# Rotary partners by small transfers on the chip in place of a permutation product

## The chip, the cores and the metric

The kernel runs on one core of one Trainium2 chip. The metric is the device time of one execution in microseconds; the time of a kernel is the median of its runs. One further execution was recorded by the hardware profiler; all rows below are from it.

## The reference, cut to what matters

Two transformer layers of width 1024 over 512 positions, the second one's input being the first one's output. The change is in the first layer's second attention branch (`differential_attention`), whose queries and keys, 4 heads with two halves of 64 dims each, get rotary positions in the first 16 of each 64 dims:

```python
def partial_rope(t, cos, sin):
    half = ROT_DIM // 2          # ROT_DIM = 16
    tf = t.astype(jnp.float32)
    t1 = tf[..., :half]
    t2 = tf[..., half:ROT_DIM]
    out = jnp.concatenate([t1 * cos - t2 * sin, t1 * sin + t2 * cos, tf[..., ROT_DIM:]], axis=-1)
    return out.astype(t.dtype)

        qb = partial_rope(q_b.reshape(b, s, 2 * H_B, HEAD_DIM), cos, sin).reshape(b, s, H_B, 2, HEAD_DIM)
        kb = partial_rope(k_b.reshape(b, s, 2 * H_B, HEAD_DIM), cos, sin).reshape(b, s, H_B, 2, HEAD_DIM)
```

The first branch (`chunked_relbias_attention`) has 8 heads in 4 units of two, with a bias by distance (the strips).

## The kernel before

All activations lie with features on the 128 partitions and the 512 positions along the row. A weight panel is 128 output features: it is loaded by SyncE (`load`), rounded on ScalarE to a high part (`split`), its remainder made on VectorE (`low`), and then multiplied in 8 steps of k with three matmuls each (`mm`). The panel's result lies in one of two PSUM banks until ScalarE evicts it (`plain`, `ropein`).

One list, `WORK`, written by `order_of_work`, holds all items, and each engine walks through it and does its own part of each item, in that order, waiting on semaphores. So the list's order is the order on every engine's queue, SyncE's too. `project` puts a panel's matmuls into it, after the fourth of them (`flush_at=3`) what is in `later`, and steps of the side work (`run(side, ...)`) between: with `STEPS_B = 2` one step after the fourth and one after the eighth. The side work is the attention units: `unit_a(0..3)` (first branch), then `unit_b(4..7)` (second). One step of a unit holds, for tile i: `norm` of tile i-1 (VectorE), `value` of tile i-3 (TensorE), two `score` products with their mask (VectorE adds the strip or mask and takes the maximum), two `turn` transposes (TensorE, copied by ScalarE) and two `exp` (ScalarE).

Panels 0 to 11 belong to units 0 to 3. Panels 12 to 23 belong to units 4 to 7, three each: query, key, value. The queries and keys, panels 12, 13, 15, 16, 18, 19, 21 and 22, take the rotary step (`rope_home` names the tile in place of the panel). While they run, the side work is unit 1 (panels 12 to 14), unit 2 (15 to 17) and unit 3 (18 to 23).

The rotary step of panel n stands in `WORK` in the middle of panel n+1, behind `low` of panel n+4:

```python
        n = project("w_in", 8 + u, STEPS_B)
        do("ropein", n)
        later.append(lambda n=n: do("rope", n))
```

TensorE multiplies the evicted panel with a 128 x 128 permutation `perm` that has the partner's place and the sign (line 1194), into a bank of ring T (banks 4 and 5, shared with the turns). VectorE multiplies that bank with the sine's table into a tile g (line 1879), POOL multiplies the panel with the cosine's table (line 2444), and VectorE adds g. The tables `COS` and `SIN` are made beforehand. The strips of the first branch (`strip`) are loaded by SyncE at the start of a unit's first step, and POOL adds the diagonal's mask to them.

Lines: 1194 matmuls, 1197 transposes, 1546 ScalarE's activations, 1879 VectorE's tensor_tensor, 1883 its tensor_scalar, 1978 its mask with maximum, 2444 POOL's tensor_tensor, 2529 SyncE's transfers.

Of the kernel before, what the change touches and what calls it, by code (L numbers as in the profile page):

```python
# [30 lines left out]

C_ID, C_PERM, C_MEAN, C_ONE, C_DIAG = range(5)
G_TRI, G_BLK, G_H0, G_H1, G_INC, G_ID, G_LEV = range(7)
# [3 lines left out]
def shape_constants():  # L37

    p = np.arange(128)[:, None]
    f = np.arange(128)[None, :]  # L40
    c = np.zeros((128, 5, 128), np.float32)
    c[:, C_ID] = p == f

    for base in (0, 64):
        for m in range(8):
            c[base + m + 8, C_PERM, base + m] = -1.0
            c[base + m, C_PERM, base + m + 8] = 1.0
    c[:, C_MEAN] = 1.0 / D
# [24 lines left out]
    inv = (np.float32(500000.0) ** (-np.arange(0, 16, 2, dtype=np.float32) / np.float32(16))).astype(np.float32)  # L73
    freq = np.where(d < 16, inv[d % 8], np.float32(0)).astype(np.float32)[:, None]
    return c.reshape(128, -1), g.reshape(128, -1), strips.reshape(128, -1), freq
# [71 lines left out]
def order_of_work():  # L147
# [4 lines left out]
    def do(*item):  # L152
        work.append(item)
# [175 lines left out]
    for u in range(4, 8):  # L329
        n = project("w_in", 8 + u, STEPS_B)  # L330
        do("ropein", n)
        later.append(lambda n=n: do("rope", n))
        n = project("w_in", 12 + u, STEPS_B)
        do("ropein", n)
        later.append(lambda n=n: do("rope", n))
        n = project("w_in", 16 + u, STEPS_B)
        do("plain", n)
        later.append(lambda u=u: start(side, unit_b, u))
# [308 lines left out]
def at(*item):  # L647

    return RANK[item]
# [43 lines left out]
for _shared, _kinds in SHARED.items():  # L693
    _count = 0
    for _item in WORK:
        for _name in _kinds.get(_item, _kinds.get(_item[0], ())):
# [5 lines left out]
RING_OF = {"panel": "P", "panelb": "P", "score": "S", "babank": "S", "baturn": "S", "vturn": "T", "turn": "T",  # L702
# [113 lines left out]
_at = 0  # L816
for _name, _n in (("soft", 96), ("freq", 1), ("lam", 8), ("lt", 128), ("sub", 1), ("half", 16), ("warm", 1), ("ss", 32),
                  ("ln", 32), ("rms", 16), ("cw", 48), ("rn", 32), ("ba", 32), ("bet", 16), ("al", 16), ("e1", 16),
                  ("w1", 16), ("gg", 16), ("ngc", 16), ("gam", 16), ("kend", 16), ("gend", 32), ("ea", 4), ("tmp1", 16),
                  ("gs", 64), ("nf", 1)):  # L820
    SM[_name] = _at
    _at += _n
# [27 lines left out]
def build(nc, a, out):  # L850

    ctx = ExitStack()
    with ctx:
        def sb(name, shape, dt=F32):
            return ctx.enter_context(nc.sbuf_tensor(name, shape, dt))
# [8 lines left out]
        Wlo = sb("Wlo", [128, HL, 1024], F32R)  # L864
        CC = sb("CC", [128, 5, 128])
        par = sb("par", [128, NP])
# [9 lines left out]

        ident, perm, mean_m, ones, diagm = (CC[:, i, :] for i in (C_ID, C_PERM, C_MEAN, C_ONE, C_DIAG))
        x2_dram = a["x2_scratch"]
# [164 lines left out]
        def let_go(item):  # L1043
# [15 lines left out]
            if kind == "turn":  # L1059
                return [(SG["pt"], at(*item))]  # L1060
            if kind == "rope":
                return [(SG["ropesin"], at(*item))]
            if kind == "feat":
# [126 lines left out]
        def tensor_engine(e):  # L1190
# [8 lines left out]
            def bank_free(*item):  # L1199
                if BEFORE[item] is not None:  # L1200
                    for s, v in let_go(BEFORE[item]):
                        w.wait_ge(s, v)

            for what, *i in WORK:
# [24 lines left out]
                elif what == "vturn":  # L1229
# [7 lines left out]
                    m.then_inc(SG["vturned"], 1)  # L1237

                elif what == "rope":
                    n, = i  # L1240
                    w.wait_ge(SG["ropein"], at("ropein", n))
                    bank_free("rope", n)
                    w.wait_ge(SG["consts"], 80)
                    mm(bank("rope", n), perm, F(rope_home(n))).then_inc(SG["permuted"], 1)

# [296 lines left out]
        def scalar_engine(e):  # L1542
# [9 lines left out]
            for what, *i in WORK:  # L1552
# [61 lines left out]
                elif what == "sin":  # L1614
                    w.wait_ge(*sig("angle", "rest", "sin"))
                    act(F(SIN), F(SIN), ACT.Sin).then_inc(SG["a_small"], 1)

# [256 lines left out]
        def vector_engine(e):  # L1874
# [24 lines left out]
            for what, *i in WORK:  # L1899
# [50 lines left out]
                elif what == "rope":  # L1950
                    n, = i
                    u, j = unit_of(n)
                    f, g = F(HOMES[u][j]), F(39 + at("rope", n) % 2)
                    w.wait_ge(SG["permuted"], at("rope", n))
                    w.wait_ge(*sig("sin", "sin"))
                    tt(g, bank("rope", n), F(SIN), ALU.mult).then_inc(SG["ropesin"], 1)
                    w.wait_ge(SG["ropesin"], at("rope", n))
# [482 lines left out]
        def pool_engine(e):  # L2440
# [9 lines left out]
            for what, *i in WORK:  # L2450
# [7 lines left out]

                elif what == "rope":
                    n, = i  # L2460
                    f = F(rope_home(n))
                    w.wait_ge(SG["permuted"], at("rope", n))
                    w.wait_ge(*sig("cos", "cos"))
                    tt(f, f, F(COS), ALU.mult).then_inc(SG["ropecos"], 1)

                elif what == "merge":
# [58 lines left out]
        def sync_engine(e):  # L2525
# [5 lines left out]
            for what, *i in WORK:  # L2531
# [18 lines left out]
                elif what == "freq":  # L2550
                    dma(SG["consts"], small("freq"), a["freq"])
                    dma(SG["consts"], F(COS).bitcast(I32), a["positions"].partition_broadcast(128))

                elif what == "strip":
# [126 lines left out]
```

## Time and profile before

| | us |
|---|---|
| median of 3 runs | 1491.37 (1489.71 to 1491.49) |
| the profiled execution | 1489.78 |
| its span | 1487.9 |
| TensorE busy | 1454.4 |
| VectorE busy | 815.9 |
| ScalarE busy | 605.9 |
| POOL busy | 135.4 |

The span is from the first to the last instruction; the profiled execution's own time is 1.88 us more. An engine's busy time is the sum of its instructions' time. Idle time is written before an instruction, with what released it. In timelines, instructions of one kind that follow each other are merged into one row with their count. An fp32 product is recorded as two matmuls (a 128 x 128 x 128 transpose too).

### The profile page before, as it was taken

To read this page: it belongs to the slowest core of one execution; us is meant where nothing else is said; L and a number is where in the kernel's file an instruction comes from. 1 tells how busy PE (TensorE), PEld (TensorE's weight loads), DVE (VectorE), ACT (ScalarE), POOL (GpSimd) and SP (SyncE) were. 2 spreads that over 40 slices of the span, in tenths; PEclk is the share of its full clock that TensorE was granted. 3 is DMA by queue.
4 is the path that set the end of the run, shared out by engine and by line. 5 is a ranking of instruction groups with operands and counts; after the bars stand their busy time and mean duration, and the time that the engine had idled before them with its cause. 6 is when DMAs were issued, how large, how long until landed. Compare 5 with 4: busy or idle time off the path is not lost.

```text
span 1487.9 us, 20042 instructions
## 1 busy us (share of the span) xinstructions
PE 1454.4 (98%) x7936; PEld 1155.8 (78%) x7936; DVE 815.9 (55%) x1422; ACT 605.9 (41%) x1096; POOL 135.4 (9%) x112
## 2 busy tenths in 40 slices
PE   7999999999999999999999999899999999999997
PEld 6776677787878888888877777687778888888886
DVE  3544455556575343444467767755664763664463
ACT  4644445542353232322336655224543432442234
POOL 0001100002200000000012000330020110110012
PEclk9999999999999999999999999999999999999999
DMA  6222221213213222232233221100232332222221
GB/s 249 71 93 74 83 68 60 71 57 113 94 40 125 96 99 100 90 108 86 99 116 113 85 72 60 55 31 16 72 114 79 106 110 89 99 100 99 83 74 57
DMA packets 39693, 130.38 MB, mean 88 GB/s; under 512 B 4656, under 2 KB 4912, under 8 KB 39600
## 3 DMA queue, kind: packets, MB, share of 16 engines
q1 hardware_dynamic: 39600, 129.09, 25.3%
q8 instruction: 64, 1.05, 0.3%
q14 instruction: 29, 0.24, 0.1%
HBM read 124.88 MB, written 4.19 MB: 87 GB/s over the span
## 4 chain that ended last, share of the span: by engine, by line
PE 88%; DVE 5%; ACT 3%; issue 2%; DMA 1%; POOL 1%; SPq 0%; POOLq 0%; DVEq 0%; ACTq 0%
PE bank L1194 85%; PE bank L1197 3%; ACT Fm L1546 2%; DVE Fm L1887 1%; DVE Wlo L1879 1%; DVE Fm L1978 1%; ACT Whi L1546 1%; DVE Fm L1879 1%; POOL Fm L2444 0%; DMA Wraw<-in_w_in_dram 0%; DMA Fm<-in_relb_dram 0%; DVE sm L1883 0%; DVE Fm L1883 0%; DVE sm L1887 0%; ACT Xr L1546 0%
## 5 line engine op out<-in xcount | busy, mean ns | idle before, releaser
L1194 PE MATMUL bank<-Rm,Whi 128*128 128x512 f32 x2816 | 872.4, 391 | 0.0
L1194 PEld LDWEIGHTS bank<-Rm,Whi 128*128 128x128 f32 x2816 | 530.8, 189 | 108.7 <-issue 0.7
L1194 PE MATMUL bank<-Rm,Wlo 128*128 128x512 f32 x1408 | 565.3, 401 | 11.8 <-DVE Rm L1879 8.0
L1879 DVE TENSOR_TENSOR Wlo<-Wraw,Whi 128x1024 fp32r<-128x1024 f32 (+1 forms) x224 | 282.4, 1263 | 171.1 <-ACT Whi L1546 170.6
L1194 PEld LDWEIGHTS bank<-Rm,Wlo 128*128 128x128 f32 x1408 | 265.7, 189 | 74.8 <-issue 19.4
L1546 ACT ACTIVATE Whi<-Wraw 128x1024 fp32r<-128x1024 f32 (+1 forms) x224 | 232.8, 1043 | 215.6 <-PE bank L1194 207.6
L1194 PE MATMUL bank<-Xr,Whi 128*128 128x512 f32 x736 | 226.6, 389 | 0.0
L2444 POOL TENSOR_TENSOR Fm<-Fm 128x512 f32<-128x512 f32 (+1 forms) x94 | 126.7, 1357 | 917.6 <-ACT Fm L1546 484.7
L1194 PEld LDWEIGHTS bank<-Xr,Whi 128*128 128x128 f32 x736 | 138.2, 188 | 28.8
L1546 ACT ACTIVATE Fm<-bank 128x512 f32<-128x512 f32 (+4 forms) x200 | 93.0, 483 | 156.0 <-PE bank L1194 105.6
L1194 PE MATMUL bank<-Xr,Wlo 128*128 128x512 f32 x368 | 143.3, 389 | 0.0
L1879 DVE TENSOR_TENSOR Fm<-Fm,bank 128x512 f32<-128x512 f32 (+2 forms) x118 | 75.9, 665 | 122.4 <-PE bank L1194 122.3
L1546 ACT ACTIVATE Fm<-Fm,sm 128x512 f32<-128x512 f32 (+3 forms) x92 | 52.9, 578 | 114.1 <-DVE sm L1883 97.5
L1546 ACT ACTIVATE Fm<-Fm 128x512 f32<-128x512 f32 (+2 forms) x116 | 61.6, 532 | 89.0 <-DVE Fm L1879 48.3
L1194 PE MATMUL bank<-Fm 128*64 128x128 f32 (+7 forms) x848 | 92.9, 318 | 4.1 <-ACT Fm L1546 1.5
L1546 ACT ACTIVATE Fm<-Fm,par 128x512 f32<-128x512 f32 x68 | 50.5, 743 | 102.4 <-DVE Fm L1879 102.4
L1194 PEld LDWEIGHTS bank<-Fm 128*64 128x64 f32 (+3 forms) x848 | 58.1, 155 | 37.8 <-issue 27.5
L1194 PEld LDWEIGHTS bank<-Xr,Wlo 128*128 128x128 f32 x368 | 69.1, 188 | 14.2
L1879 DVE TENSOR_TENSOR Fm<-Fm 128x512 f32<-128x512 f32 x63 | 44.1, 700 | 62.3 <-ACT Fm L1546 56.1
L1879 DVE TENSOR_TENSOR Fm<-bank,Fm 128x512 f32<-128x512 f32 (+1 forms) x65 | 44.4, 686 | 49.9 <-PE bank L1194 47.6
L1887 DVE SCALAR_TENSOR_TENSOR Fm<-Fm,par 128x511 f32<-128x511 f32 x88 | 65.4, 747 | 1.5
L1546 ACT ACTIVATE Rm<-Fm 128x512 fp32r<-128x512 f32 (+1 forms) x58 | 35.9, 626 | 73.1 <-POOL Fm L2444 48.1
(97 smaller groups left out, 755.9 us busy)
## 6 DMA issues: line engine op xcount, KB each, us to landing
Wraw<-in_w_in_dram SPq DMA_DIRECT2D x68, 512.0 KB, 3.2
Wraw<-in_w_ff_dram SPq DMA_DIRECT2D x64, 512.0 KB, 3.2
Wraw<-in_w_up_dram SPq DMA_DIRECT2D x44, 512.0 KB, 3.3
Wraw<-in_w_o_dram SPq DMA_DIRECT2D x16, 512.0 KB, 3.2
Wraw<-in_w_down_dram SPq DMA_DIRECT2D x16, 512.0 KB, 3.2
Wraw<-in_w_ab_dram SPq DMA_DIRECT2D x8, 512.0 KB, 3.3
Wraw<-in_w_down_end_dram SPq DMA_DIRECT2D x8, 384.0 KB, 3.0
Fm<-in_x_dram SPq DMA_DIRECT2D x8, 256.0 KB, 6.1
```

Source lines behind the costliest of these rows:

```text
L1194: return e.matmul(o, l, r, start=first, stop=last)
L1197: return e.transpose(o, x, ident)
L1546: return e.activation(o, x, func, **kw)
L1879: return e.tensor_tensor(o, x, y, op)
L1887: return e.scalar_tensor_tensor(out=o, in0=x, scalar=s, in1=y, op0=op0, op1=op1)
L1978: e.tensor_tensor_reduce(p, bank("score", u, j)[:, 0:n], strip[:, 512 - n:512], 1.0, LOW, ALU.add, ALU.max, mx).then_inc(SG["masked"], 1)
L2444: return e.tensor_tensor(o, x, y, op)
```

## The change

The sign goes from the permutation into the sine: the column `freq` gets a second column with -1 for the first 8 of each 64 dims and 1 elsewhere, which ScalarE's Sin takes as its scale. The partners (rows 0 to 7 from 8 to 15, and back, and the same from 64 on) are copied from the evicted panel's tile to g by four transfers of 8 rows x 512, 16 KB each, issued by SyncE (`ropeswap`), right behind the eviction in `WORK`. g's other rows keep finite values of earlier contents, which meet a sine of zero. VectorE then does all three operations. TensorE's product and POOL's step go, ring T serves the turns alone, and the constants lose one 128 x 128 block. Tiles 39 and 40 alternate as g; they hold angles before, so the first two swaps wait for the sine's table, and later ones for the rotary step two before.

```diff
-C_ID, C_PERM, C_MEAN, C_ONE, C_DIAG = range(5)
+C_ID, C_MEAN, C_ONE, C_DIAG = range(4)
...
-    freq = np.where(d < 16, inv[d % 8], np.float32(0)).astype(np.float32)[:, None]
+    freq = np.stack([np.where(d < 16, inv[d % 8], np.float32(0)), np.where(d < 8, -1, 1)], 1).astype(np.float32)
...
         n = project("w_in", 8 + u, STEPS_B)
         do("ropein", n)
+        do("ropeswap", n)
         later.append(lambda n=n: do("rope", n))
         n = project("w_in", 12 + u, STEPS_B)
         do("ropein", n)
+        do("ropeswap", n)
         later.append(lambda n=n: do("rope", n))
...
-                elif what == "rope":
-                    n, = i
-                    w.wait_ge(SG["ropein"], at("ropein", n))
-                    bank_free("rope", n)
-                    w.wait_ge(SG["consts"], 80)
-                    mm(bank("rope", n), perm, F(rope_home(n))).then_inc(SG["permuted"], 1)
...
-                    act(F(SIN), F(SIN), ACT.Sin).then_inc(SG["a_small"], 1)
+
+                    act(F(SIN), F(SIN), ACT.Sin, scale=small("freq", 1)).then_inc(SG["a_small"], 1)
...
                     f, g = F(HOMES[u][j]), F(39 + at("rope", n) % 2)
-                    w.wait_ge(SG["permuted"], at("rope", n))
-                    w.wait_ge(*sig("sin", "sin"))
-                    tt(g, bank("rope", n), F(SIN), ALU.mult).then_inc(SG["ropesin"], 1)
+                    w.wait_ge(*sig("cos", "cos"))
+                    r = at("rope", n)
+                    w.wait_ge(SG[f"swapped{r % 2}"], 64 * ((r + 1) // 2))
+                    tt(g, g, F(SIN), ALU.mult).then_inc(SG["ropesin"], 1)
+                    tt(f, f, F(COS), ALU.mult).then_inc(SG["ropecos"], 1)
                     w.wait_ge(SG["ropesin"], at("rope", n))
                     w.wait_ge(SG["ropecos"], at("rope", n))
                     tt(f, f, g, ALU.add).then_inc(SG["roped"], 1)
...
-                elif what == "rope":
-                    n, = i
-                    f = F(rope_home(n))
-                    w.wait_ge(SG["permuted"], at("rope", n))
-                    w.wait_ge(*sig("cos", "cos"))
-                    tt(f, f, F(COS), ALU.mult).then_inc(SG["ropecos"], 1)
...
+                elif what == "ropeswap":
+
+                    n, = i
+                    r = at("ropeswap", n)
+                    w.wait_ge(SG["ropein"], at("ropein", n))
+                    if r < 3:
+                        w.wait_ge(*sig("sin", "sin"))
+                    else:
+                        w.wait_ge(SG["roped"], r - 2)
+                    f, g = F(rope_home(n)), F(39 + r % 2)
+                    for to, of in ((0, 8), (8, 0), (64, 72), (72, 64)):
+                        dma(SG[f"swapped{r % 2}"], g[to:to + 8, :], f[of:of + 8, :])
```

On SyncE's queue, from the last constants to the strips of unit 3 (`in_relb` are the strips), before:

```order
L2529 DMA Fm<-in_strips_dram 128x512
L2529 DMA Wraw<-in_w_in_dram 128x1024 [waits s_w_lo,s_w_hi] x4
L2529 DMA Fm<-in_relb_dram 128x512 [waits s_masked]
L2529 DMA Fm<-in_relb_dram 128x512
L2529 DMA Wraw<-in_w_in_dram 128x1024 [waits s_w_lo,s_w_hi] x4
L2529 DMA Fm<-in_relb_dram 128x512 [waits s_masked]
```

The same queue now, the part from the strips of unit 2 to those of unit 3 (swaps of panels 15, 16 and 18):

```order
L2513 DMA Fm<-in_relb_dram 128x512
L2513 DMA Fm<-Fm 8x512 [waits s_roped,s_ropein]
L2513 DMA Fm<-Fm 8x512 x3
L2513 DMA Wraw<-in_w_in_dram 128x1024 [waits s_w_lo,s_w_hi]
L2513 DMA Fm<-Fm 8x512 [waits s_roped,s_ropein]
L2513 DMA Fm<-Fm 8x512 x3
L2513 DMA Wraw<-in_w_in_dram 128x1024 [waits s_w_lo,s_w_hi] x2
L2513 DMA Fm<-Fm 8x512 [waits s_roped,s_ropein]
L2513 DMA Fm<-Fm 8x512 x3
L2513 DMA Wraw<-in_w_in_dram 128x1024 [waits s_w_lo,s_w_hi]
L2513 DMA Fm<-in_relb_dram 128x512 [waits s_masked]
```

The four transfers of a panel stand ahead of the weight load that had followed, and those of panel 18 and one load directly ahead of the strips of unit 3; each group waits for its panel's eviction.

On VectorE's queue, the rotary step of panel 15 with its low half ahead and the norm and masks of unit 2 behind, before:

```order
L1879 TENSOR_TENSOR Wlo<-Wraw,Whi 128x1024 [waits s_w_hi]
L1879 TENSOR_TENSOR Fm<-bank,Fm 128x512 [waits s_permuted]
L1879 TENSOR_TENSOR Fm<-Fm 128x512 [waits s_ropecos,s_ropesin]
L1987 RECIPROCAL sm<-sm 128x2 [waits s_exped]
L1883 TENSOR_SCALAR Fm<-Fm,sm 128x128 [waits s_v_step]
L1883 TENSOR_SCALAR Fm<-Fm,sm 128x128
L1978 ISA Fm,sm<-bank,Fm 128x256 [waits s_turned,s_scored]
```

And now:

```order
L1868 TENSOR_TENSOR Wlo<-Wraw,Whi 128x1024 [waits s_w_hi]
L1868 TENSOR_TENSOR Fm<-Fm 128x512 [waits s_swapped1]
L1868 TENSOR_TENSOR Fm<-Fm 128x512
L1868 TENSOR_TENSOR Fm<-Fm 128x512 [waits s_ropecos,s_ropesin]
L1978 RECIPROCAL sm<-sm 128x2 [waits s_exped]
L1872 TENSOR_SCALAR Fm<-Fm,sm 128x128 [waits s_v_step]
L1872 TENSOR_SCALAR Fm<-Fm,sm 128x128
L1969 ISA Fm,sm<-bank,Fm 128x256 [waits s_turned,s_scored]
```

The step waits for the swap in place of TensorE, and has one operation more, the cosine's product, in place of the wait for POOL.

## Rows read from the trace of the kernel before

**Rows 1.** The page, busy time of each engine (share of the span) and instructions.
```profile
PE 1454.4 (98%) x7936; PEld 1155.8 (78%) x7936; DVE 815.9 (55%) x1422; ACT 605.9 (41%) x1096; POOL 135.4 (9%) x112
```

**Rows 2.** Constants' tile on TensorE, 95 to 200 us: count, ns min/median/max, starts.
```profile
L1194 PE MATMUL bank<-Fm,CC x16: 590/591/697, 99.9 to 191.3; 128*128 128x512 f32 x16
```

**Rows 3.** TensorE's timeline: start, duration (us), work [idle before <-releaser].
```profile
99.89 1.12 PE L1194 MATMUL bank<-Fm,CC 128*128 128x512 f32 x2 [0.41 <-ACT Fm L1546]
...
110.88 0.88 PE L1194 MATMUL bank<-Fm 128*64 128x128 f32 x12
...
125.90 1.02 PE L1194 MATMUL bank<-Fm,CC 128*128 128x512 f32 x2
126.85 0.70 PE L1194 MATMUL bank<-Fm 64*128 64x256 f32 x4
...
130.43 1.22 PE L1194 MATMUL bank<-Fm 64*128 64x384 f32 x4
131.59 0.44 PE L1197 MATMUL bank<-CC,Fm 128*128 128x128 f32 x2
...
135.90 1.12 PE L1194 MATMUL bank<-Fm,CC 128*128 128x512 f32 x2 [1.12 <-ACT Fm L1546]
...
145.99 0.60 PE L1197 MATMUL bank<-CC,Fm 128*128 128x128 f32 x4
...
166.51 1.23 PE L1194 MATMUL bank<-Fm 64*128 64x384 f32 x4
...
171.99 0.66 PE L1197 MATMUL bank<-CC,Fm 128*128 128x128 f32 x4 [1.13 <-ACT Fm L1546]
```

**Rows 4.** ScalarE's timeline, evictions behind the exps.
```profile
107.72 1.33 ACT L1546 ACTIVATE Fm<-bank 128x384 f32<-128x384 f32 x3
...
124.69 0.58 ACT L1546 ACTIVATE Fm<-bank 128x512 f32<-128x512 f32 x1
...
143.73 1.33 ACT L1546 ACTIVATE Fm<-bank 128x384 f32<-128x384 f32 x3
...
151.22 0.60 ACT L1546 ACTIVATE Fm<-bank 128x512 f32<-128x512 f32 x1 [2.12 <-PE bank L1194]
```

**Rows 5.** VectorE's timeline, rotary step of panel 15 and a mask.
```profile
127.38 0.68 DVE L1879 TENSOR_TENSOR Fm<-bank,Fm 128x512 f32<-128x512 f32 x1
128.72 0.69 DVE L1879 TENSOR_TENSOR Fm<-Fm 128x512 f32<-128x512 f32 x1 [0.65 <-POOL Fm L2444]
129.33 0.16 DVE L1987 RECIPROCAL sm<-sm 128x2 f32<-128x2 f32 x1
...
129.92 0.41 DVE L1978 CUSTOM_DVE_ANT_0 Fm<-bank,Fm 128x256 f32<-128x256 f32 x1
...
159.23 0.29 DVE L1978 CUSTOM_DVE_ANT_0 Fm<-bank,Fm 128x128 f32<-128x128 f32 x1 [0.27 <-PE bank L1194]
```

**Rows 6.** SyncE's timeline of transfer issues: two constants, one weight load.
```profile
7.07 0.44 SPq L2529 DMA_DIRECT2D par<-in_par_dram  x1
7.55 0.44 SPq L2529 DMA_DIRECT2D rowp<-in_rows_dram  x1
...
85.84 0.33 SPq L2529 DMA_DIRECT2D Wraw<-in_w_in_dram  x1
```

**Rows 7.** Transfers by source: count, KB each, median us from issue to landing.
```profile
Wraw<-in_w_in_dram SPq DMA_DIRECT2D x68, 512.0 KB, 3.2
...
Wraw<-in_w_down_end_dram SPq DMA_DIRECT2D x8, 384.0 KB, 3.0
...
Fm<-in_relb_dram SPq DMA_DIRECT2D x8, 256.0 KB, 3.9
x_scratch<-Fm SPq DMA_DIRECT2D x8, 256.0 KB, 2.0
...
out_dram<-Fm SPq DMA_DIRECT2D x8, 256.0 KB, 2.5
```

**Rows 8.** Constants' tile on POOL, whole run: the bias strips' masks.
```profile
L2444 POOL TENSOR_TENSOR Fm<-Fm,CC x8: 456/460/913, 34.5 to 157.8; 128x128 f32<-128x128 f32 x8
```

More of the change, by code:

```diff
@@ L40, in shape_constants @@
     f = np.arange(128)[None, :]
-    c = np.zeros((128, 5, 128), np.float32)
+    c = np.zeros((128, 4, 128), np.float32)
     c[:, C_ID] = p == f
[L44 to L47, printed above, removed]
     c[:, C_MEAN] = 1.0 / D
@@ L816 @@
 _at = 0
-for _name, _n in (("soft", 96), ("freq", 1), ("lam", 8), ("lt", 128), ("sub", 1), ("half", 16), ("warm", 1), ("ss", 32),
+for _name, _n in (("soft", 96), ("freq", 2), ("lam", 8), ("lt", 128), ("sub", 1), ("half", 16), ("warm", 1), ("ss", 32),
                   ("ln", 32), ("rms", 16), ("cw", 48), ("rn", 32), ("ba", 32), ("bet", 16), ("al", 16), ("e1", 16),
@@ L864, in build @@
         Wlo = sb("Wlo", [128, HL, 1024], F32R)
-        CC = sb("CC", [128, 5, 128])
+        CC = sb("CC", [128, 4, 128])
         par = sb("par", [128, NP])
@@ L875, in sig @@
             return SG[shared], value
-        ident, perm, mean_m, ones, diagm = (CC[:, i, :] for i in (C_ID, C_PERM, C_MEAN, C_ONE, C_DIAG))
+        ident, mean_m, ones, diagm = (CC[:, i, :] for i in (C_ID, C_MEAN, C_ONE, C_DIAG))
         x2_dram = a["x2_scratch"]
@@ L1060, in let_go @@
                 return [(SG["pt"], at(*item))]
-            if kind == "rope":
-                return [(SG["ropesin"], at(*item))]
             if kind == "feat":
@@ L2550, in sync_engine @@
                 elif what == "freq":
-                    dma(SG["consts"], small("freq"), a["freq"])
+                    dma(SG["consts"], small("freq", 0, 2), a["freq"])
                     dma(SG["consts"], F(COS).bitcast(I32), a["positions"].partition_broadcast(128))
+                elif what == "ropeswap":
[9 more added lines that the diff above has]
+                        dma(SG[f"swapped{r % 2}"], g[to:to + 8, :], f[of:of + 8, :])
                 elif what == "strip":
```

2 rows, old and new, of the table RING_OF are left out of this document.

## The prediction

> **What bounds the kernel now.** Read the page first, then the engines' timelines between 96 and 196 us, where all eight rotary steps lie. TensorE is busy 98% of the span [rows 1]: what is taken from its queue shortens the run, unless something it waits for comes no earlier. Each rotary step costs it one fp32 product, recorded as two matmuls, 16 in this stage [rows 2]. Where it waits for nothing, one is started at 125.90 and the scores behind it at 126.85: 0.95 us each [rows 3].
>
> But this stage is not bound by TensorE alone. A head unit (scores, mask on VectorE, exp on ScalarE, normalising on VectorE, turn on TensorE, copy on ScalarE, value) runs as side work, one step in the middle and one at the end of each panel, and that chain is nearly as long as the products it hides behind. The reader is to see this at three kinds of place. Before two permutations TensorE sat idle 0.41 and 1.12 us, since ScalarE evicts the panel behind the exp; before the turn at 171.99 it was 1.13 us [rows 3]. At 130.43 the score pair took 1.16 us to the next start (131.59), because the second one's bank was still being masked, and at 166.51 the pair is recorded with the same 1.2 us [rows 3, 5]. And at 145.99 the turn of the values came 0.9 us after its panel's eviction, the last of three operations from 143.73 [rows 3, 4].
>
> **What goes.** Eight products of 0.95 us are 7.6 us, and the two waits of 0.41 and 1.12 stand before removed products: 9.1 us at most. POOL's eight steps hid beside VectorE, save for the 0.65 us that VectorE waited for each [rows 5].
>
> **What comes on VectorE.** Before: sine product at 127.38, wait for POOL, sum at 128.72, next operation at 129.33: 1.95 us [rows 5]. Now three operations in a row. Two are spaced 0.61 us (128.72 to 129.33), the sum waits for its neighbour's end and a semaphore, 0.69 + 0.05: together 1.96 us. So the third operation costs nothing; it fills the hole where POOL was waited for. What this hides behind is only that hole: VectorE is otherwise no later.
>
> **What comes before it: the swap.** The old product needed the eviction at once, the new step needs four transfers. The first waits on SyncE for the eviction, so from the eviction's end (125.27) it is: 0.1 us to the first issue (as a mask ends at 130.33 and the scores it releases start at 130.43) [rows 3, 5]; three further issues, spaced 0.47 as the constants are (7.07, 7.55), 1.41 us; and the last one's landing [rows 4, 6]. No transfer of 16 KB within the chip is in the trace. Nearest are the 256 KB stores, 2.0 us and 2.5 us from issue. From 512 KB to 384 KB the time falls by 0.2 us, so 240 KB less may save 0.4: 1.6 us from below. From above 3.0 us, the 384 KB load [rows 7]. Issues as short as the single load's 0.33 us aren't excluded either [rows 6]. The swap then lands L = 0.1 + 1.0 + 1.6 = 2.7 us after the eviction at least, 0.1 + 1.41 + 3.0 = 4.5 at most; I take 1.8 for the landing, between its lower bound and the fastest row, since the size is small and the nearest row is 2.0: L = 3.3.
>
> VectorE would be ready for it 2.11 us after the eviction (125.27 to 127.38: the split on ScalarE, then the low half). So where the rotary step comes right behind these two, it now ends later by d = L - 2.1 = 1.2 us (0.6 to 2.4), and all of the unit's chain queued behind it with it: norm, masks, negation, and so exp and the next eviction on ScalarE. That is the case for panels 12, 15, 16, 19 (and 13, with nothing of the chain behind it). For 18, 21 and 22 nothing that TensorE waits for is queued behind the step in time (the headout's sums, or the masks of a pair that comes half a panel later); there it costs nothing.
>
> [...]
>
> **The sum, by the units of side work.** Times are those of before; I carry along how far TensorE is off.
> Unit 1 (panels 12 to 14). TensorE saves 0.41 + 0.95 at panel 12 and 0.95 at 13. But the value product after the second (110.88) needs the copy of a turn, the second of the three ScalarE operations from 107.72, done at 108.6 (two of 0.44), now 108.6 + d. Room is 2.28 - d: it comes 1.08 us earlier instead of 2.3 [rows 3, 4].
> Unit 2 (panels 15 to 17). The scores at 130.43 wait for the first mask (it starts at 129.92) and the turns at 131.59 were already held by the second: both are d later, in spite of the 0.95 saved. Eviction 16 is d late, its swap too, and rotary step 16 ends 2d late; exp and the eviction of panel 17 with it, 145.06 + 2d. The turn of the values at 145.99 can't start before: 2d - 0.93 = +1.47 us. The 0.95 and the 1.12 of panel 16 are lost in this wait [rows 3, 4, 5].
> Unit 3 (panels 18 to 22). At 18 TensorE saves 0.95, but the mask of the first scores now waits for the bias strips: they are issued behind swap 18 (eviction 151.8, + 0.1, four issues 1.9, a weight load 0.4, so 154.1 and 154.6), land 3.9 us later [rows 7], and with POOL's masks of 0.46 us, the first beside the second landing [rows 8], VectorE starts at about 159.3, where it was 159.23 [rows 5]: +0.1. So the chain is no earlier, step 19 makes it d later, the turn behind 166.51 is d + 0.1 late; the wait at 171.99, for ScalarE, shows that it stays so. Steps 21 and 22 then pay in full, 1.90 us: d + 0.1 - 1.9 = -0.6 us.
> Together 4d - 5.0 us, and with d = 1.2: -0.2 us. Beyond 196 us nothing differs, TensorE carries its place on.
> The profiled execution, 1489.78 us with 1487.9 of span, would be 1489.6. The median of the runs is 1.6 above it, so I forecast 1491.2 us. About 0.2%, 3 us, is what a measurement here can tell from no change.
>
> Weight loads: load n+7 went out when low half n+3 was made, mid-panel; behind a swap it goes about half a panel, 5 us, later. It lands 3.2 us after [rows 7] and its split is due three panels, over 20 us, on. Nothing. The smaller constants and the sign in ScalarE's scale (a column instead of a number) are nothing.
>
> **Rivals.**
> A, the swap is quick or the chain has slack that I don't see: with L near the 2.1 us at which VectorE is ready, d is 0 and the sum -5.0: 1486.4 us. [...] Against: three further issues alone take 1.0 to 1.4 us. Chance 0.20, the cases down to d = 0.5 included.
> B, the product's whole price comes out: -9.1, 1482.3 us. It needs the masks and exps not to bind TensorE. For it: three waits of TensorE, 2.66 us, are all that the stage shows as idle [rows 3]. Against: the places at 130.43, 166.51 and 171.99, where the chain binds already. Chance 0.10.
> C, slower: the swap becomes the bound. The load queued right behind each swap moves 512 KB at the same time as the last of its small copies. With the landing at 3.0 us, L is 4.5, d 2.4, the sum +4.6: 1496.0 us. It decides from d = 1.25 on (no gain) and is measurable from d = 2.0, L = 4.1. For it: unit 2 pays it twice, since its second step waits behind its first. Against: the stores' medians are 2.0 and 2.5 us [rows 7]. Chance 0.16.
> My forecast, d from 0.5 to 2.0, has 0.54; its own range is 1488.2 to 1494.2. The range for 8 in 10 takes in d = 0 and stops short of C's full price: 1486 to 1495.5. Faster by over 0.2%: A and B, 0.30; within: 0.54; slower: 0.16.
>
> **What would show it.** SyncE issuing groups of four, 0.47 apart, with 1.8 us to landing; VectorE idle about 1.2 us ahead of the sine product in panels 13, 16, 17 and 20, and its three operations in 1.96 us; TensorE with no 128x512 permutation, but new waits for a mask at the end of panels 16 and 20 and for ScalarE in the middle of 18. If these waits are absent and the stage ends 7 us or more earlier, my chain has slack and B is right. If VectorE waits over 2 us for each swap, C is. A late weight load (TensorE waiting for a low half from 125 to 200 us) would refute the last paragraph of the sum.

## The result and the profile after

| | us |
|---|---|
| before, median of 5 | 1490.85 (1487.42 to 1491.49) |
| changed, median of 5 | 1497.64 (1493.89 to 1497.92) |
| ratio changed / before | 1.0039, 95% interval 1.0024 to 1.0054 |
| profiled execution, changed | 1497.64, span 1495.9 |

The change makes the kernel slower by 0.4%. The forecast was no change, 1491.2 us, and the time lies above its range of 1486 to 1495.5 us.

The page of the changed kernel, its span and its busy times, against [rows 1]:

```profile
span 1495.9 us, 20036 instructions
...
PE 1454.0 (97%) x7920; PEld 1158.1 (77%) x7920; DVE 820.9 (55%) x1430; ACT 605.5 (40%) x1096; POOL 122.4 (8%) x104
```

TensorE has 16 matmuls fewer, and the span is 8.0 us longer. TensorE's timeline with its waits (start, duration, work, idle time before and its releaser), the rows that answer to [rows 3]:

```profile
99.55 1.50 PE L1189 MATMUL bank<-Fm 128*64 128x128 f32 x8
...
106.83 0.88 PE L1192 MATMUL bank<-CC,Fm 128*128 128x128 f32 x6 [1.84 <-DVE Fm L1872]
...
110.89 0.88 PE L1189 MATMUL bank<-Fm 128*64 128x128 f32 x12 [0.43 <-ACT Fm L1534]
...
126.00 0.70 PE L1189 MATMUL bank<-Fm 64*128 64x256 f32 x4
...
132.40 1.25 PE L1189 MATMUL bank<-Fm 64*128 64x384 f32 x4 [2.73 <-DVE sm L1969]
133.58 0.63 PE L1192 MATMUL bank<-CC,Fm 128*128 128x128 f32 x2
...
144.58 0.88 PE L1192 MATMUL bank<-CC,Fm 128*128 128x128 f32 x6 [0.85 <-DVE Fm L1872]
...
149.12 0.66 PE L1192 MATMUL bank<-CC,Fm 128*128 128x128 f32 x4 [0.90 <-ACT Fm L1534]
...
172.44 1.99 PE L1189 MATMUL bank<-Fm 64*128 64x384 f32 x4 [4.42 <-DVE sm L1969]
174.36 0.69 PE L1192 MATMUL bank<-CC,Fm 128*128 128x128 f32 x2
...
179.11 0.60 PE L1192 MATMUL bank<-CC,Fm 128*128 128x128 f32 x4
...
199.86 0.49 PE L1189 MATMUL bank<-Fm 64*128 64x128 f32 x4
```

The same instructions in the kernel before, where [rows 3] do not have them, and the scores at which the stage is entered (95.43) and those behind its last rotary step (201.97):

```profile
95.43 0.92 PE L1194 MATMUL bank<-Fm 64*128 64x384 f32 x4
...
142.50 0.88 PE L1197 MATMUL bank<-CC,Fm 128*128 128x128 f32 x6
...
167.67 0.44 PE L1197 MATMUL bank<-CC,Fm 128*128 128x128 f32 x2
...
194.57 0.49 PE L1194 MATMUL bank<-Fm 64*128 64x128 f32 x4
...
201.97 0.92 PE L1194 MATMUL bank<-Fm 64*128 64x384 f32 x4
```

Set against the same instruction of before, TensorE's place is: +0.01 us at 110.89, -0.85 at 126.00, +1.97 at 132.40, +2.08 at 144.58, +3.13 at 149.12, +5.93 at 172.44, +6.69 at 174.36, +7.12 at 179.11 and, for the scores behind all eight steps (194.57 before, 199.86 now), +5.29. There are no permutations, but waits of 1.84, 0.43, 2.73, 0.85, 0.90 and 4.42 us that were not there. Four of them stand where the prediction looked for a late chain: 0.43 (the copy of a turn), 2.73 and 4.42 (masks, at the ends of panels 16 and 20) and 0.90 (the eviction, in the middle of 18). Those of 1.84 and 0.85, turns that wait for a norm, it did not name. SyncE's issues, VectorE's rotary step of panel 15 and the first mask of unit 3, against [rows 5] and [rows 6]:

```profile
125.30 2.67 SPq L2513 DMA_DIRECT2D Fm<-Fm  x4
...
158.24 0.91 SPq L2513 DMA_DIRECT2D Fm<-in_relb_dram  x2
```

```profile
129.32 1.29 DVE L1868 TENSOR_TENSOR Fm<-Fm 128x512 f32<-128x512 f32 x2 [1.84 <-DMA Fm<-Fm]
...
163.22 0.29 DVE L1969 CUSTOM_DVE_ANT_0 Fm<-bank,Fm 128x128 f32<-128x128 f32 x1 [1.46 <-POOL Fm L2435]
```

Four copies take 2.67 us to issue, one every 0.67 to 0.69 us, where the constants were 0.48 apart (7.07 to 7.55; the prediction has 0.47). The last is issued at 127.35 and VectorE begins at 129.32, 1.97 us on. ScalarE's eviction ends at 125.27, as it did before, so the swap lands 4.05 us after it, L = 4.1, and VectorE stands still 1.84 us ahead of the step (1.82 to 1.97 us at all eight); its three operations take 2.00 us (the next starts at 131.32). Ready at 127.38 before and starting at 129.32 now, VectorE is late by d = 1.95 us.

The granted clock of TensorE in four stretches (columns: stretch and length, busy us and count of PE, PEld, DVE, ACT, POOL, then PEclk, DMA share and GB/s), changed, and under it the last two stretches of before:

```profile
125.00:151.00 26.00, 21.52 (x109) 14.97 (x108) 13.96 (x36) 10.39 (x25) 0.00 (x0) 0.93 0.20 67
151.00:200.00 49.00, 44.58 (x236) 33.09 (x236) 22.38 (x52) 17.96 (x39) 0.92 (x2) 0.93 0.23 76
355.00:385.00 30.00, 27.13 (x107) 21.87 (x107) 13.88 (x14) 4.74 (x6) 4.79 (x3) 0.89 0.24 85
950.00:980.00 30.00, 26.07 (x376) 20.27 (x376) 20.25 (x64) 7.73 (x17) 18.74 (x20) 0.94 0.11 37
```

```profile
355.00:385.00 30.00, 27.13 (x113) 21.97 (x112) 13.49 (x15) 5.46 (x7) 4.36 (x4) 0.94 0.25 85
950.00:980.00 30.00, 26.03 (x488) 21.46 (x488) 19.54 (x49) 7.66 (x18) 19.74 (x22) 1.00 0.13 44
```

Before had 1.00 in the first two stretches, which is full speed. Now it is 0.93 in both: the granted clock is 0.50 from 134.0 to 137.0 us, behind the wait of 2.73 us, and from 171.5 to 178.0, from before the end of the wait of 4.42 us on; at 133 and at 179 us it is 1.00. The pair of scores at 172.44 takes 1.99 us where it took 1.23. The last two stretches lie outside the change. There both kernels have the same pauses of TensorE (2.87 us of idle time ahead of one matmul at about 365 to 370 us in each, and 2.30 and 2.33 us ahead of one at about 963 to 970), and the clock around them differs from one profiled execution to the next: that of the changed kernel was at 0.50 twice (369.5 to 376.0 and 970.0 to 973.0 us), that of before once and more briefly (365.0 to 368.0), that of changed_again (below) not at all. It is worth 1.2 us between the scores above (+5.29) and 415 us (+6.52), and 1.5 us more at 970 us (+8.02). So of the 8.0 us some 5.2 belong to the changed stage, and 2.7 to the two pauses, in this pair of executions.

### The profile page after: what moved, and what is told of

Same layout as the page of the kernel before. It is cut to its first block, busy times and chain, and to the rows that moved or that the text cites. A ratio compares the mean times of both kernels' runs of the same rounds, so it can differ in the third digit from the quotient of the medians.

```text
span 1495.9 us, 20036 instructions
## 1 busy us (share of the span) xinstructions
PE 1454.0 (97%) x7920; PEld 1158.1 (77%) x7920; DVE 820.9 (55%) x1430; ACT 605.5 (40%) x1096; POOL 122.4 (8%) x104
## 4 chain that ended last, share of the span: by engine, by line
PE 87%; DVE 5%; ACT 3%; issue 2%; DMA 1%; SPq 1%; POOL 0%; POOLq 0%; DVEq 0%; ACTq 0%
PE bank L1189 84%; PE bank L1192 3%; ACT Fm L1534 2%; DVE Fm L1876 1%; DVE Fm L1969 1%; DVE Fm L1868 1%; DVE Wlo L1868 1%; SPq L2513 1%; ACT Whi L1534 1%; DMA Fm<-Fm 1%; DMA Wraw<-in_w_in_dram 0%; DVE sm L1872 0%; DMA Fm<-in_relb_dram 0%; POOL Fm L2435 0%; DVE sm L1876 0%
## 5 line engine op out<-in xcount | busy, mean ns | idle before, releaser
L2435 POOL TENSOR_TENSOR Fm<-Fm 128x512 f32<-128x512 f32 (+1 forms) x86 | 114.1, 1335 | 863.8 <-ACT Fm L1534 484.6
L1868 DVE TENSOR_TENSOR Fm<-Fm 128x512 f32<-128x512 f32 x79 | 54.3, 695 | 72.6 <-ACT Fm L1534 56.2
L1868 DVE TENSOR_TENSOR Fm<-bank,Fm 128x512 f32<-128x512 f32 (+1 forms) x57 | 38.9, 687 | 45.5 <-PE bank L1189 43.2
```

Of the source, the lines that this page charges most:

```text
L1868: return e.tensor_tensor(o, x, y, op)
L2435: return e.tensor_tensor(o, x, y, op)
```

## The experiments

Each ran beside the kernel before on the same chip; its ratio is to those runs. Theory 1: the swap's latency, that is the four issues in a row and the last landing, makes VectorE late, and the chain of side work multiplies it. Theory 2: another part of the change costs the time (the third operation on VectorE, the ring of banks, SyncE's order).

**no_swap.** The copies out, and SyncE's waits with them; VectorE waits for the eviction and the sine's table alone:

```diff
+                    w.wait_ge(*sig("sin", "sin"))
...
-                    w.wait_ge(SG[f"swapped{r % 2}"], 64 * ((r + 1) // 2))
+                    w.wait_ge(SG["ropein"], at("ropein", n))
...
-                        dma(SG[f"swapped{r % 2}"], g[to:to + 8, :], f[of:of + 8, :])
```

> Leaves out the partners' copies (the rotated numbers are not the reference's); all else is the changed kernel. Theory 1, the swap's latency: in the changed kernel it lands 4.1 us after the eviction, VectorE stands still 1.9 us ahead of each rotary step, and the chain of side work multiplies that. Without it d = 0 and the formula 4d - 5.0 gives 5 us less than before, about 1486; TensorE waits for no mask over 1 us and its clock does not fall between 125 and 200 us. Theory 2, another edit loses the time (the third operation on VectorE, ring T, SyncE's order): the time stays at 1495 or above.

Measured: 1484.69 us (1481.02 to 1486.04), ratio 0.9966 (0.9954 to 0.9978), 5.4 us under the 1490.10 of before: the 5.0 of the formula. Its two waits for masks (the second row shows three of its four matmuls, where its view ends):

```profile
129.07 1.25 PE L1189 MATMUL bank<-Fm 64*128 64x384 f32 x4 [0.80 <-DVE sm L1970]
...
163.54 0.93 PE L1189 MATMUL bank<-Fm 64*128 64x384 f32 x3 [0.80 <-DVE sm L1970]
```

TensorE waits for no mask over 1 us, as expected, and the clock was 1.00 from 120 to 200 us. Theory 2 is refuted for the third operation, the ring of banks and the tables, which are all in this kernel; SyncE's order went with the copies, and one_transfer and strip_first are for it. And the products' price of 9.1 us does not come out even here: the chain gives no more.

**one_transfer.** One copy of the four:

```diff
-                    w.wait_ge(SG[f"swapped{r % 2}"], 64 * ((r + 1) // 2))
+                    w.wait_ge(SG[f"swapped{r % 2}"], 16 * ((r + 1) // 2))
...
-                    for to, of in ((0, 8), (8, 0), (64, 72), (72, 64)):
+                    for to, of in ((0, 8),):
```

> One copy of 8 rows in place of four (three quarters of the partners are left out). Theory 1: the three further issues at 0.69 us go, the swap lands 0.1 + 2.0 = 2.1 us after the eviction, as VectorE comes free, so d = 0 and the time is within 1.5 us of no_swap, about 1486. Rival, the landing itself is slow because the copy's size or the load behind it delays it: VectorE still waits about 1.9 us for it, and the time is within 2 us of the changed kernel's 1497.

Measured: 1484.41 us (1483.21 to 1486.87), ratio 0.9966 (0.9956 to 0.9977). SyncE's issue of the copy of panel 15, and VectorE's low half and rotary step:

```profile
124.78 0.65 SPq L2513 DMA_DIRECT2D Fm<-Fm  x1
```

```profile
125.74 1.23 DVE L1868 TENSOR_TENSOR Wlo<-Wraw,Whi 128x1024 fp32r<-128x1024 f32 x1 [2.38 <-ACT Whi L1534]
126.88 1.29 DVE L1868 TENSOR_TENSOR Fm<-Fm 128x512 f32<-128x512 f32 x2
```

The step starts as soon as the low half is done, with no wait: a copy of 16 KB is there within 2.1 us of its issue. So the landing alone makes nobody wait; the three further issues do. One copy also moves a quarter of the bytes; the next run keeps the bytes and doubles the issues.

**eight_transfers.** The same rows in eight copies of four:

```diff
-                    w.wait_ge(SG[f"swapped{r % 2}"], 64 * ((r + 1) // 2))
+                    w.wait_ge(SG[f"swapped{r % 2}"], 128 * ((r + 1) // 2))
...
-                        dma(SG[f"swapped{r % 2}"], g[to:to + 8, :], f[of:of + 8, :])
+                        for p in (0, 4):
+                            dma(SG[f"swapped{r % 2}"], g[to + p:to + p + 4, :], f[of + p:of + p + 4, :])
```

> The same rows in eight copies of 4 rows. Theory 1: four further issues at 0.69 us, the swap lands 6.9 us after the eviction, VectorE waits 4.7 us, d = 4.8; by the formula's slope 4 x 2.8 = 11 us more than the changed kernel, about 1508, and more waits long enough for TensorE's clock to fall. If the issues overlap with the landing (Theory 1b) or the swap is not what counts (Theory 2): within 3 us of the changed kernel.

Measured: 1509.54 us (1508.09 to 1511.04), ratio 1.0137 (1.0122 to 1.0153). Issues, VectorE's step and three of TensorE's waits (the view ends within these rows: in full, the transposes' six matmuls take 1.54 us and the four of each pair of scores 1.99):

```profile
130.74 4.95 SPq L2513 DMA_DIRECT2D Fm<-Fm  x8
```

```profile
136.97 1.29 DVE L1868 TENSOR_TENSOR Fm<-Fm 128x512 f32<-128x512 f32 x2 [4.05 <-DMA Fm<-Fm]
```

```profile
110.22 1.11 PE L1192 MATMUL bank<-CC,Fm 128*128 128x128 f32 x4 [4.09 <-DVE Fm L1872]
...
140.05 1.65 PE L1189 MATMUL bank<-Fm 64*128 64x384 f32 x3 [4.94 <-DVE sm L1969]
...
186.83 1.00 PE L1189 MATMUL bank<-Fm 64*128 64x384 f32 x1 [7.27 <-DVE sm L1969]
```

The issues are 0.62 us apart here, VectorE waits 4.05 us, d is 4.1 to 4.2. The formula gives 4 x 4.15 - 5.0 = 11.6 us over before; it is 19.4. So it gets the direction and some 60% of the size; what is above it comes with waits of 4 to 7 us, each followed by work at a granted clock of 0.50, which reads so from 109.0 to 115.5, 140.0 to 146.0 and 184.0 to 190.5 us (scores of 1.99 us, transposes of 1.54 instead of 0.88). That the expected 1508 us was nearly met is partly luck: d was expected at 4.8, too long, and the formula's four times is too little.

**late_rope.** The changed kernel with the rotary step half a panel later, behind the panel's second side step:

```diff
-        later.append(lambda n=n: do("rope", n))
+        later.append(lambda n=n: behind.append(lambda: do("rope", n)))
...
         run(side, steps - steps * (many - 1) // many)
+        while behind:
+            behind.pop(0)()
```

> The changed kernel, with the rotary step placed behind the panel's second step of side work, half a panel later. Theory 1: VectorE has no wait ahead of norm and masks, the swap has landed long before, and the products' whole price comes out, 9.1 us below before, 1482; the strips of unit 3 still come 2 us late and may cost 1 to 2 us of it. Theory 2: no better than the changed kernel minus 2 us, since its operations are the same.

Measured: 1481.38 us (1479.13 to 1481.89), ratio 0.9945 (0.9930 to 0.9960), 8.7 us under before. The rotary step of panel 15 and what follows on VectorE, and TensorE's only two waits from 90 to 215 us:

```profile
128.01 2.09 DVE L1870 TENSOR_TENSOR Fm<-Fm 128x512 f32<-128x512 f32 x3
130.91 1.23 DVE L1870 TENSOR_TENSOR Wlo<-Wraw,Whi 128x1024 fp32r<-128x1024 f32 x1 [0.81 <-ACT Whi L1536]
```

```profile
157.83 1.25 PE L1191 MATMUL bank<-Fm 64*128 64x384 f32 x4 [0.62 <-DVE sm L1971]
...
163.33 0.66 PE L1194 MATMUL bank<-CC,Fm 128*128 128x128 f32 x4 [1.12 <-ACT Fm L1536]
```

The same four copies are now awaited by nobody (the step at 128.01 starts without a wait), and nearly all of the 9.1 us is there.

**strip_first.** The changed kernel, the strips of unit 3 loaded ahead of the copies of panel 18:

```diff
         n = project("w_in", 8 + u, STEPS_B)
         do("ropein", n)
+        if u == 6:
+            do("stripload", 3)
         do("ropeswap", n)
...
     def unit_a(u):
+        if u < 3:
+            do("stripload", u)
         do("strip", u)
...
-                elif what == "strip":
+                elif what == "stripload":
```

> The changed kernel with the load of unit 3's bias strips issued ahead of the copies of panel 18 instead of behind them. Theory 1 with strips: VectorE's first mask of unit 3 waited for them until 163.22, 1.5 us; they come 2.7 us earlier, so TensorE's longest wait (4.42 us at 172.44) falls by about 1.5 us, and the half clock behind it may shrink with it: 1.5 to 3.5 us below the changed kernel, 1494 to 1496. Rival, the strips are hidden and step 19's swap alone makes that wait: no change, 1497.

Measured: 1492.93 us (1491.29 to 1498.66), ratio 1.0028 (1.0013 to 1.0043): 2.3 and 4.7 us less than the changed kernel's two medians. Against before on its own chip it is 3.1 us slower, where those two were 5.1 and 6.8; the intervals of the three ratios overlap, so that the traces have to decide. POOL's strip masks in the changed kernel, then VectorE's first mask and TensorE's wait without the delay (the last row shows two of the pair's four matmuls, where its view ends: the four take 1.99 us; the granted clock is 0.50 from 171.0 to 173.5):

```profile
161.95 0.46 POOL L2435 TENSOR_TENSOR Fm<-Fm,CC 128x128 f32<-128x128 f32 x1 [40.84 <-DMA Fm<-in_relb_dram]
162.59 0.45 POOL L2435 TENSOR_TENSOR Fm<-Fm,CC 128x128 f32<-128x128 f32 x1 [0.18 <-DMA Fm<-in_relb_dram]
```

```profile
160.56 0.68 DVE L1872 TENSOR_TENSOR Rm<-bank,Rm 128x512 fp32r<-128x512 f32 x1
161.16 0.28 DVE L1973 CUSTOM_DVE_ANT_0 Fm<-bank,Fm 128x128 f32<-128x128 f32 x1
```

```profile
170.39 1.35 PE L1193 MATMUL bank<-Fm 64*128 64x384 f32 x2 [2.87 <-DVE sm L1973]
```

In the changed kernel the first mask (163.22) waited 1.46 us for POOL. Here it follows the headout's sum without a pause, and the wait of 4.42 is 2.87. So the strips, and not the swap of panel 19 alone, make that wait longer. The clock is 0.97 from 151 to 200 us in place of 0.93. The stage is 1.2 us shorter than in the changed kernel's profiled execution and 1.9 us shorter than in changed_again's (table below); what the medians show above that is not shown to be the strips'.

**cos_on_vector.** The kernel before with POOL's step given to VectorE:

```diff
                     tt(g, bank("rope", n), F(SIN), ALU.mult).then_inc(SG["ropesin"], 1)
+                    w.wait_ge(*sig("cos", "cos"))
+                    tt(f, f, F(COS), ALU.mult).then_inc(SG["ropecos"], 1)
```

> The kernel before (permutation product kept) with the cosine's product moved from POOL to VectorE. Theory 1: the third operation fills the hole in which VectorE waited for POOL; 1.96 against 1.95 us per step; same time as before within 1 us. Theory 2, it lengthens the chain by 0.6 us per step: the formula's 4 x 0.6 gives +2.4 us.

Measured: 1490.21 us against 1489.84, ratio 1.0001 (0.9992 to 1.0011). VectorE's step, against [rows 5]:

```profile
126.58 0.69 DVE L1879 TENSOR_TENSOR Fm<-bank,Fm 128x512 f32<-128x512 f32 x1
127.18 1.48 DVE L1879 TENSOR_TENSOR Fm<-Fm 128x512 f32<-128x512 f32 x2
128.57 0.16 DVE L1989 RECIPROCAL sm<-sm 128x2 f32<-128x2 f32 x1
```

1.99 us from the sine's product to the next operation, where it was 1.95 with the pause for POOL. The third operation is free, as worked out.

**two_queues.** The changed kernel, two copies issued by SyncE and two by POOL:

```diff
-                    w.wait_ge(SG[f"swapped{r % 2}"], 64 * ((r + 1) // 2))
+                    w.wait_ge(SG[f"swapped{r % 2}"], 32 * ((r + 1) // 2))
+                    w.wait_ge(SG[f"pswapped{r % 2}"], 32 * ((r + 1) // 2))
...
-                    for to, of in ((0, 8), (8, 0), (64, 72), (72, 64)):
+                    for to, of in ((0, 8), (8, 0)):
...
+                    for to, of in ((64, 72), (72, 64)):
+                        e.dma_start(g[to:to + 8, :], f[of:of + 8, :]).then_inc(SG[f"pswapped{r % 2}"], 16)
```

> The changed kernel with two of the four copies issued by SyncE and two by POOL. Theory 1, the issues in a row are what makes the swap late: if POOL's issue takes no longer than SyncE's 0.69 us, it lands 0.1 + 0.7 + 2.0 = 2.8 us after the eviction, d = 0.7, 4d - 5.0 = -2.2 us against before, 1488. If POOL's two land later than SyncE's four did (over 4.1 us), the time is that of the changed kernel or more, and the wait on VectorE tells POOL's own time.

Measured: 1489.49 us (1486.74 to 1492.43), ratio 0.9999 (0.9988 to 1.0010). POOL's issues and VectorE's step of panel 15:

```profile
123.83 1.05 POOL L2461 DMA_DIRECT2D Fm<-Fm  x2 [5.48 <-ACT Fm L1534]
```

```profile
126.41 2.09 DVE L1868 TENSOR_TENSOR Fm<-Fm 128x512 f32<-128x512 f32 x3 [0.67 <-DMA Fm<-Fm]
```

The wait of 1.84 us is 0.67, as expected from two issues instead of four, and the loss is gone; of the 2.2 us of gain that the formula gives there are 0.35. The strips still come behind two copies (VectorE's first mask of unit 3 waits 1.98 us for POOL), and the wait for the masks of unit 3 (3.27 us at 167.23) still ends in slow scores: 1.99 us, with the granted clock at 0.50 from 167.5 to 170.5.

**late_product.** The kernel before with its whole rotary step moved as in late_rope (the edit is the same).

> The kernel before with its rotary step (product, POOL's step and VectorE's) moved behind the panel's second step of side work, as in late_rope. It parts late_rope's gain: the place alone should take the waits of 0.41 and 1.12 us ahead of two products and the VectorE time ahead of the masks, 1.5 to 2.5 us, 1488; the eight products, 7.6 us, stay, so that late_rope is 6 to 8 us faster than this. Rival, the place alone does it: within 2 us of late_rope.

Measured: 1489.77 us (1487.28 to 1492.17), ratio 0.9996 (0.9987 to 1.0005). TensorE ahead of two of the moved products:

```profile
107.84 1.10 PE L1196 MATMUL bank<-Fm,CC 128*128 128x512 f32 x2 [0.74 <-ACT Fm L1548]
...
132.80 1.10 PE L1196 MATMUL bank<-Fm,CC 128*128 128x512 f32 x2 [0.35 <-ACT Fm L1548]
```

In the medians the place alone gives nothing, where 1.5 to 2.5 us were expected. The profiled execution says otherwise: from the entry of the stage to the scores behind it, it takes 104.88 us where before took 106.54, 1.7 us less (table below), and it loses that again by a later start and by lower granted clocks from 355 to 385 and from 950 to 980 us (0.89 and 0.94, before 0.94 and 1.00). The interval of the ratio, 1.9 us less to 0.7 more, allows both, so what the place alone is worth stays open. The product now stands right behind an eviction that waits for the exp, and TensorE waits 0.74 and three times 0.35 us there, 1.8 us in all against 2.66 before. The gain of late_rope over this one is 7 us by the stages and 8 by the medians, near the 7.6 us of the eight products, and needs both the product gone and the step out of the chain's way.

**late_strip.** late_rope and strip_first together.

> late_rope with the strips of unit 3 issued ahead of the copies as in strip_first. In late_rope TensorE's only waits in the stage are 0.62 us at the scores of unit 3 and 1.12 us for the eviction of panel 20. With the strips 2.7 us earlier the first may go: 0 to 0.7 us below late_rope, 1481. If both gains of the single changes added (8.7 + 4.4 us), it would be 1477.

Measured: 1478.91 us (1478.36 to 1481.88), ratio 0.9933 (0.9919 to 0.9946): 11.3 us under before, the fastest kernel here. Its only wait from 90 to 215 us:

```profile
164.30 0.66 PE L1198 MATMUL bank<-CC,Fm 128*128 128x128 f32 x4 [0.41 <-ACT Fm L1540]
```

It is 3.3 us under late_rope_again, where 0 to 0.7 was expected. Its gain of 11.3 us is also more than the 9.1 that the prediction set as the most the change can give: the third wait of before, 1.13 us at 171.99, stands before no product and was not counted, and it is 0.41 here. TensorE is 1.9 us ahead of it at this row and 3.7 at 400 us; the second part of that is a fall of the clock that the profiled late_rope_again had (0.50 from 359.0 to 361.0 us, 0.96 from 350 to 390) and this one had not (1.00). Why the eviction ahead of this row is earlier by more than the mask was stays open.

**changed_again** and **late_rope_again**, on the same chip as late_strip:

> The changed kernel itself once more, on the same chip as late_strip and late_rope_again, for a comparison on common ground: 6 to 7 us over before, and between 1493 and 1498 with the granted clock lower where the time is longer.

> late_rope once more: 8 to 9 us under before, 15 us under the changed kernel.

Measured: 1495.22 us (1492.90 to 1498.71), ratio 1.0042 (1.0027 to 1.0057), 5.1 us over the 1490.16 of before, where 6 to 7 were expected. The executions at a granted clock of 0.996 take 1492.9 and 1494.0 us, those at 0.990 and 0.992 take 1498.7 and 1498.3. In the profiled one the stage is lost as before (waits of 3.51 and 4.88 us), and the clock is 1.00 at both later pauses: its span is 1491.1 us, not 1495.9. late_rope_again: 1482.26 us (1479.30 to 1482.50), ratio 0.9947 (0.9934 to 0.9961), 7.9 us under before and 13.0 under changed_again, a little less than expected on both counts.

**The stage alone.** The profiled executions enter the stage up to 3 us apart and differ again at the two later pauses, whatever the change. The length from the scores at the entry to the third pair of scores behind the stage (95.43 and 201.97 in before) leaves both out:

| run | enters, us | leaves, us | stage against before, us | medians against before, us |
|---|---|---|---|---|
| before | 95.43 | 201.97 | (106.54) | |
| changed | 95.58 | 207.26 | +5.1 | +6.8 |
| changed_again | 94.68 | 207.05 | +5.8 | +5.1 |
| no_swap | 96.26 | 197.25 | -5.6 | -5.4 |
| one_transfer | 97.14 | 198.39 | -5.3 | -5.7 |
| two_queues | 95.00 | 201.14 | -0.4 | -0.4 |
| eight_transfers | 96.72 | 222.69 | +19.4 | +19.4 |
| strip_first | 93.83 | 204.27 | +3.9 | +3.1 |
| cos_on_vector | 94.59 | 201.26 | +0.1 | +0.4 |
| late_product | 96.88 | 201.76 | -1.7 | -0.1 |
| late_rope | 93.92 | 191.54 | -8.9 | -8.7 |
| late_rope_again | 96.53 | 194.45 | -8.6 | -7.9 |
| late_strip | 96.63 | 192.51 | -10.7 | -11.3 |

With d of 0, 0.7, 1.95 and 4.15 us the stage is -5.3 to -5.6, -0.4, +5.1 to +5.8 and +19.4 us. That is 5.5 to 7.4 us for each us of d, not the formula's four.

## Why the prediction was wrong

**Right.** The mechanism. The stage is bound by the side work's chain; the swap makes VectorE late by d, the masks, exps and evictions carry it on, unit 2 takes it twice. Measured with d = 1.95: TensorE is 0.1 us ahead at the end of unit 1 (formula: 2.28 - d = 0.33), 3.1 us behind through unit 2 (2d - 0.93 = 2.97). With d = 0 the whole is -5.4 us (formula -5.0). VectorE's third operation is free (cos_on_vector; the forecast's 0.05 us for the semaphore is an estimate that no row shows: in the changed kernel the third starts at 130.72, 0.10 us behind the second's end, and the three take 2.00 us against 1.96), TensorE waits for no low half from 125 to 200 us, so the weight loads are not late, and steps 21 and 22 pay in full: +7.12 becomes +5.29. My rival C, the swap as the bound, is what happened in kind, with L = 4.1; its own sign, VectorE waiting over 2 us for each swap, was just missed (1.82 to 1.97 us).

**Wrong: the term "three further issues, spaced 0.47 as the constants are, 1.41 us".** The spacing is 0.69 us. The copies of 8 rows take 0.62 to 0.65 us to issue, and the constants' 0.44 did not carry over to them. Over three issues that is some 0.6 us. The landing, taken at 1.8, is 1.97, and at most 2.1 in one_transfer. Together L is 4.1 in place of 3.3, d is 1.95 in place of 1.2, and four times 0.75 us is 3.0 us of the miss. By itself this leaves the sum at +2.8 us, about 1494.2 us and still inside the range; it takes the next two terms to leave it.

**Wrong: "So the chain is no earlier", +0.1 us for the strips of unit 3.** The same spacing holds back the strips: issued at 158.24, masked by POOL until 163.04. Their place is 0.8 us later than before, relative to TensorE, in place of 0.1: 0.7 us.

**Missing: the clock.** The sum counted nothing for it and took TensorE's speed as given. With the two long waits the granted clock falls to 0.50. At the scores of unit 3 that is 0.76 us (1.92 us to the next start instead of 1.16), and 0.43 us more by the turn at 179.11. The sum was -0.2; +3.0, +0.7 and +1.2 make 4.7 us. The stage measures 5.15 (5.29 less the 0.14 us that this execution was late before the first step); 0.45 us are not accounted for. Behind the wait of 2.73 us, too, the matmuls from 133.58 to 138.30 took 1.4 us more than at a clock of 1.00 (4.72 us, where before took 3.30 without the permutation and its wait). I count nothing for them, since the turn at 149.12 waited for ScalarE even so; no run tests that. The formula holds at d = 0 and says too little wherever VectorE waits for the copies, in two_queues with its 0.67 us too.

The first pair of medians is 6.8 us apart, the second 5.1, which is 1495.22 us and just inside the range. In the profiled pair, 8.0 us apart, the rest is the clock at the two later pauses, where executions differ; for the medians, of which there are no traces, that is likely but not shown: the changed kernel's first five had a mean granted clock of 0.991 to 0.994, changed_again's had 0.990 to 0.996. Whether the change makes these later falls more frequent, by where they come in time, stays open.

The chances gave 0.16 to slower and 0.54 to no change. The error was to take the issue of a transfer of another shape as known: I widened the landing upwards and the spacing only downwards. With 0.69 and my landing of 1.8, L is 4.0 and d 1.9, a sum of +2.6 us, at the threshold of C.

## What to carry to other kernels

The transfers on the chip that stand here in place of a product take no time of TensorE's own, but they put 1.97 us of landing and 0.69 us for each further issue into what waits for them. Before such transfers go in, look at what is queued behind the waiting instruction, and move that instruction behind the work that others wait for: here the same four copies lose 5 us in one place and win 9 in another, half a panel later. An engine that is busy 98% was still held by a chain here, and a delay in this chain counted once for every link in which it came again, and more: 5.5 to 7.4 us for each us of d. The waits of 2.73 us and more that this stage has, in five runs, all came with a granted clock of 0.50 as well.

## What the runs showed of the hardware

- SyncE's issue of an SBUF to SBUF copy of 8 rows x 2 KB takes 0.62 us in the changed kernel (0.76 the first), 0.69 from one to the next, and 0.65 alone in one_transfer. One of 4 rows takes 0.58 in eight_transfers, 0.62 from one to the next, 4.95 for eight: half the rows save 0.05 to 0.07 us an issue. The load of 512 KB takes 0.33 to 0.39 in the changed kernel. POOL issues two copies in 1.05 us in two_queues.
- Such a copy is usable 1.97 us after its issue in the changed kernel, and within 2.1 us in one_transfer.
- With a wait of TensorE of 2.73 us (to 132.40) and one of 4.42 us (to 172.44) in the changed kernel came a granted clock of 0.50, 134.0 to 137.0 and 171.5 to 178.0 us; with one of 1.84 us (to 106.83) it stayed at 1.00, and the transposes behind it take their usual 0.88 us. The length of the wait alone does not decide it: in strip_first one of 1.83 us (to 105.08) came with 0.50 from 106.0 to 109.0, and behind the same 2.87 us of idle time at about 370 us the next matmul takes 0.76 us in the changed kernel's execution and 0.47 in changed_again's.
